# Down product of a feed-forward by seven block products instead of eight, with the second half of the tokens handed on first

## The reference

```
gate, up = jnp.split(xn @ w_gate_up[l], 2, axis=-1)
x = x + (jax.nn.silu(gate) * up) @ w_down[l]        # (1024 x 2816) @ (2816 x 1024)
return rms_norm(x, final_norm_g)
# second block, start
hc = modulate(rmsnorm(ctx, norm1_g), csh1, csc1)    # 256 context tokens
hx = modulate(rmsnorm(x, norm1_g), sh1, sc1)
q_x, k_x, v_x, ... = split(hx @ w_in)               # k_c, v_c of the context from hc
```

## Time and profile before

| | us |
|---|---|
| median of 3 runs | 3002.29 (3001.2 to 3003.21) |
| the profiled execution | 3003.17, its span 3001.1 |
| TensorE, VectorE, ScalarE, GpSimd busy in it | 2849.3, 1757.3, 1299.1, 512.4 |
| gate-up product | up to 970.6 |
| down product | 970.6 to 1212.2 |
| entry of the second block up to q | 1212.2 to some 1293 |

### The profile page before, as it was taken

How to read it: one execution, slowest core, us unless ns; L and a number is a source line. 1 busy time by engine, 2 the same in 40 slices (tenths; PEclk the granted TensorE clock), 3 DMA queues, 4 the chain that set the end, 5 groups by cost and what they waited for, 6 DMA issues and landing times.

```text
span 3001.1 us, 34761 instructions
## 1 busy us (share of the span) xinstructions
PE 2849.3 (95%) x14050; PEld 2269.2 (76%) x14050; DVE 1757.3 (59%) x2366; ACT 1299.1 (43%) x1809; POOL 512.4 (17%) x424
## 2 busy tenths in 40 slices
PE   6999998999999999899999999999999579999997
PEld 5777776788778888788888676666888368888885
DVE  4344534788775333843323555555355669999997
ACT  4344433333333223311111666665223357777775
POOL 0011102555554000421000111111000200000000
PEclk8999999999999999999999999999999789999998
DMA  3210131345654531221211111114324569999996
GB/s 106 85 43 29 43 105 71 96 137 155 189 155 152 197 102 49 84 65 43 74 60 36 50 40 43 40 43 152 102 98 169 224 224 386 398 391 398 398 397 238
DMA packets 239619, 439.79 MB, mean 147 GB/s; under 512 B 27436, under 2 KB 134068, under 8 KB 238948
## 3 DMA queue, kind: packets, MB, share of 16 engines
q1 hardware_dynamic: 217184, 359.69, 34.2%
q0 software_dynamic: 22128, 77.85, 7.5%
q10 hardware_dynamic: 148, 0.04, 0.0%
HBM read 383.96 MB, written 53.58 MB: 146 GB/s over the span
## 4 chain that ended last, share of the span: by engine, by line
PE 90%; DVE 6%; ACT 2%; issue 1%; DMA 0%; ACTq 0%; POOL 0%; POOLq 0%; DVEq 0%
PE PS L125 84%; PE PS L128 5%; DVE m L134 3%; ACT m L131 2%; DVE m L140 1%; ACT L131 0%; DVE m L176 0%; DVE m L143 0%; DVE m L179 0%; DVE m L173 0%; DMA m<-xh_scratch,small 0%; DVE m L137 0%; ACTq L182 0%; DVE small L134 0%; DMA out_dram<-m 0%
## 5 line engine op out<-in xcount | busy, mean ns | idle before, releaser
L125 PE MATMUL PS<-m,m 128*128 128x512 f32 (+4 forms) x12234 | 2662.7, 391 | 45.4 <-DVE m L134 24.2
L125 PEld LDWEIGHTS PS<-m,m 128*128 128x128 f32 (+2 forms) x12234 | 2064.9, 184 | 567.7 <-issue 121.9
L131 ACT ACTIVATE m<-m 128x2048 fp32r<-128x2048 f32 (+4 forms) x600 | 705.1, 1191 | 881.5 <-PE PS L125 507.8
L134 DVE TENSOR_TENSOR m<-m,m 128x2048 fp32r<-128x2048 f32 (+5 forms) x576 | 852.1, 1500 | 366.3 <-ACT m L131 337.3
L131 ACT ACTIVATE m<-PS 128x512 f32<-128x512 f32 (+4 forms) x503 | 279.4, 578 | 515.7 <-PE PS L125 336.4
L134 DVE TENSOR_TENSOR m<-PS,m 128x512 fp32r<-128x512 f32 (+1 forms) x360 | 235.8, 685 | 344.6 <-PE PS L125 301.1
L134 POOL TENSOR_TENSOR m<-m,m 128x512 f32<-128x512 f32 (+3 forms) x166 | 264.7, 1597 | 646.2 <-DVE small L143 208.3
L128 PE MATMUL PS<-ident,m 128*128 128x128 f32 x1592 | 225.1, 281 | 84.0 <-DVE m L149 36.0
L128 PEld LDWEIGHTS PS<-ident,m 128*128 128x128 f32 x1592 | 193.9, 145 | 122.9 <-DVE m L149 36.2
L131 ACT ACTIVATE m<-m,small 128x640 f32<-128x640 f32 (+4 forms) x199 | 156.3, 788 | 220.7 <-DVE small L137 155.2
L143 DVE CUSTOM_DVE_ANT_0 m<-PS,m 128x640 f32<-128x640 f32 (+4 forms) x192 | 146.4, 775 | 118.5 <-PE PS L125 118.5
(11 more groups left out here) (80 smaller groups left out, 451.2 us busy)
## 6 DMA issues: line engine op xcount, KB each, us to landing
m<-in_w_exp_gate_dram SPq DMA_DIRECT2D x64, 1024.0 KB, 8.6
m<-in_w_exp_up_dram SPq DMA_DIRECT2D x64, 1024.0 KB, 8.8
m<-in_w_exp_down_dram SPq DMA_DIRECT2D x64, 1024.0 KB, 8.2
m<-in_w_mod_dram SPq DMA_DIRECT2D x48, 512.0 KB, 3.7
m<-in_w_gate_up_dram SPq DMA_DIRECT2D x44, 512.0 KB, 6.4
m<-in_w_in_dram SPq DMA_DIRECT2D x41, 512.0 KB, 4.1
m<-in_w_in_dram SPq DMA_DIRECT2D x12, 1024.0 KB, 5.1
h_scratch<-m POOLq DMA_DIRECT2D x22, 512.0 KB, 3.2
```

Of the source, the lines that this page charges most:

```text
L125: return Unsent() if self.e is None else self.e.matmul(o, l, r, start=first, stop=last, **k)
L131: return Unsent() if self.e is None else self.e.activation(o, i, fn, **k)
L134: return Unsent() if self.e is None else self.e.tensor_tensor(o, a, b, op)
```

## The change

The down product is also done by seven block products. h^T is cut in A11, A12, A21, A22 (token half by hidden half) and w_down in B11 to B22 (hidden half by column half); each block product P is 11 steps of 128 hidden rows, 4 token tiles x 3 matmuls of 512 columns each, in the order P1 P2 P5 P6 P7 P4 P3. P2 adds onto P1 in the same banks and P3 onto P5.

Every step takes two pieces of 128x512, one of h and one of w. Those that are plain blocks come through two rings of eight places of 256 KB (`h_slot`, `w_slot`). The others are sums, made by GpSimd (`dn_sum`): S1 = A21 + A22, S2 = S1 - A11, S3 = A11 - A21, S4 = A12 - S2 and T1 = B12 - B11, T2 = B22 - T1, T3 = B22 - B12, T4 = T2 - B21, eleven tiles each. S1, S2, S4 live in `s_all`, T1, T2, T4 in `t_all`; A21 and B12 are first loaded there whole (2.9 MB each). S3 and T3 are made in the ring's places. The splits go to rings of four (`hs`, `ws`): both of step n wait for the matmuls of step n - 4. A place of the ring is loaded again when the split or the sum that reads it is done.

VectorE adds the results (`dn_result`) after the splits of certain steps, up to two steps past the product's end, and holds U2 and U3 in `dU2`, `dU3`; GpSimd adds U3 into x for one block. C22 and C21, the second half of the tokens, are done before P3, whose result C12 is of the first half. So the norm of tiles 4 to 7 is made during P3, and the second block's entry takes the tiles in the order 4 5 6 7 0 1 2 3 (`X_ORDER`), with the first two k2 products and four value products on the second half. The k weights of the second block are loaded early and split during P3. Loads that move: x is read back right after the gate-up's end, the rows and tables later.

```diff
+        DN_ORDER = "P1 P2 P5 P6 P7 P4 P3".split()
...
+        dU2, dU3 = ar(134, 4, 512), ar(86, 4, 512)
+        H_RING = ([("A11", t, "P1") for t in range(11)] + [(b, t, r) for t in range(11) for b, r in (("A12", "P2"), ("A22", "S1"))]
+                  + [("A11", t, "S2") for t in range(11)] + [(b, t, r) for t in range(11) for b, r in (("A11", "P7"), ("A21", "S3"))]
+                  + [("A22", t, "P4") for t in range(11)] + [("A12", t, "S4") for t in range(11)])
+        W_RING = ([("B11", t, "P1") for t in range(11)] + [("B21", t, "P2") for t in range(11)] + [("B22", t, "T2") for t in range(11)]
+                  + [(b, t, r) for t in range(11) for b, r in (("B22", "P7"), ("B12", "T3"))] + [("B21", t, "T4") for t in range(11)])
...
+        def h_ring_load(sp, j):
+            b, t, r = H_RING[j]
+            c = t + 11 * (b[2] == "2")
+            sp.wait_ge(f"h_st{c % 2}", c)
+            if j >= 8:
+                _, t_, r_ = H_RING[j - 8]
+                if r_[0] == "P":
+                    sp.wait_ge("h_low", dn_step(r_, t_), "A")
+                else:
+                    sp.wait_ge("dn_sum", r_, t_)
+            sp.dma_start(h_slot[j % 8], h_block(b, t, 1)).then_inc(*sp.landed(f"h_in{j % 8}", "d", j))
+        def w_ring_load(sp, j):
+            b, t, r = W_RING[j]
+            if j >= 8:
+                _, t_, r_ = W_RING[j - 8]
+                if r_[0] == "P":
+                    sp.wait_ge("h_low", dn_step(r_, t_), "B")
+                if r_ == "P1":
+                    sp.wait_ge("dn_sum", "T1", t_)
+                if r_[0] == "T":
+                    sp.wait_ge("dn_sum", r_, t_)
+            sp.dma_start(w_slot[j % 8], w_block(b, t, 1)).then_inc(*sp.landed(f"wd_in{j % 8}", "d", j))
...
+            sp.wait_ge("w_low", W_GU + 21)
+            for t in range(8):
+                h_ring_load(sp, t)
+                w_ring_load(sp, t)
+        def down_sp(sp):
             sp.wait_ge("gu_acc", 21, "P7")
...
+            sp.dma_start(t_all, w_block("B12", 0, 11).rearrange("(t p) n -> p t n", p=128)).then_inc(*sp.landed("ct_in"))
+            for t in range(8, 11):
+                h_ring_load(sp, t)
+                w_ring_load(sp, t)
+            for t in range(11):
+                if t == 1:
+                    sp.wait_ge("gu_acc", 21, "P4")
+                    sp.wait_ge("gu_up", 21, "C12")
+                    sp.wait_ge("h_st0", 20)
+                    sp.wait_ge("h_st1", 21)
+                    sp.dma_start(s_all, h_block("A21", 0, 11).rearrange("(t p) n -> p t n", p=128)).then_inc(*sp.landed("cs_raw"))
+                h_ring_load(sp, H_AT["P2", t])
+                w_ring_load(sp, W_AT["P2", t])
+                h_ring_load(sp, H_AT["S1", t])
+            for t in range(11):
+                h_ring_load(sp, H_AT["S2", t])
+                w_ring_load(sp, W_AT["T2", t])
+            for t in range(11):
+                h_ring_load(sp, H_AT["P7", t])
+                h_ring_load(sp, H_AT["S3", t])
+                w_ring_load(sp, W_AT["P7", t])
+                w_ring_load(sp, W_AT["T3", t])
+            for t in range(11):
+                w_ring_load(sp, W_AT["T4", t])
+                h_ring_load(sp, H_AT["P4", t])
+            for t in range(11):
+                h_ring_load(sp, H_AT["S4", t])
+                if t == 2:
+                    sp.wait_ge("dn_sum", "T4", 10)
+                    for t_ in range(4):
+                        w_last_load(sp, t_)
+                    w_load(sp, W_V2)
+            for t in range(4, 11):
+                w_last_load(sp, t)
+            sp.wait_ge("h_low", 76, "B")
+            sp.dma_start(sinT, sin_t).then_inc(*sp.landed("cs_in"))
+            sp.wait_ge("md_turned", "x", 4, 4)
+            sp.wait_ge("h2_sum", 1, 3)
             sp.dma_start(cosT, cos_t).then_inc(*sp.landed("cs_in"))
...
         def down_pe(pe):
-            for n, (c, kg, k0, kk) in enumerate(dn_pairs):
-                W = W_DN + 6 * c + kg
-                H, L = w_split(W)
-                hi, lo = hsp[n % 2]
-                pe.wait_ge("h_low", n)
-                pe.wait_ge("w_low", W)
-                for i in range(NT):
-                    if n % 11 == 0:
-                        pe.take(i, "x2_half", c, i)
-                    for k in range(2):
-                        ks = kk + k
-                        t = mm3(pe, PS[:, i, :], (hi[:, k, tile128(i)], lo[:, k, tile128(i)]), (H[:, ks, :], L[:, ks, :]),
-                                n % 11 + k == 0, k0 + ks == 21)
-                    t.then_inc(*pe.did("dn_acc", n, i))
-                    if n == 21 and i >= 3 and i < 7:
-                        _, a, k0_ = md_parts[i - 3]
+            for P in DN_ORDER:
+                added = P in ("P2", "P3")
+                for t in range(11):
+                    n = dn_step(P, t)
+                    (ah, al), (bh, bl) = hs[n % 4], ws[n % 4]
+                    pe.wait_ge("h_low", n, "B")
+                    for i in range(4):
+                        b = dn_bank(P, i)
+                        if t == 0:
+                            pe.take(b, *(("dn_s1", i) if P == "P1" else ("x2_half", DN_TAKEN[P], i)))
+                        mm3(pe, PS[:, b, :], (ah[:, tile128(i)], al[:, tile128(i)]), (bh, bl), t == 0 and not added, t == 10,
+                            **(dict(skip_group_check=True) if added else {})).then_inc(*pe.did("dn_acc", n, i))
+                    if P == "P3" and 4 <= t < 8:
+                        _, a, k0 = md_parts[t - 4]
                         pe.wait_ge("cx_shifted", a)
-                        pe.turn = i - 3
-                        turn4(pe, cx[:, a, :], k0_, 4, "md_turned", ("c", a, k0_), ("md_low", md_no["c", a, k0_]))
-                w_done[W] = ("dn_acc", n, 7)
-            pe.turn = 4
+                        pe.turn = t - 4
+                        turn4(pe, cx[:, a, :], k0, 4, "md_turned", ("c", a, k0), ("md_low", md_no["c", a, k0]))
+            pe.turn = 0
...
+        def dn_highs(act, n):
+            for x, ring in (("A", hs), ("B", ws)):
+                v, ready = dn_source(n, x)
+                act.wait_ge(*ready)
+                if n >= 4:
+                    act.wait_ge("dn_acc", n - 4, 3)
+                else:
+                    act.wait_ge("gu_acc", 21, "P1" if x == "A" else "P2")
+                act.activation(ring[n % 4][0], v, ACT.Copy).then_inc(*act.did("h_high", n, x))
+        def dn_lows(dve, n):
+            for x, ring in (("A", hs), ("B", ws)):
+                H, L = ring[n % 4]
+                dve.wait_ge("h_high", n, x)
+                dve.tensor_tensor(L, dn_source(n, x)[0], H.bitcast(F32), ALU.subtract).then_inc(*dve.did("h_low", n, x))
...
+            results = {24: "C11", 46: "U2", 48: "U2_in", 57: "U3", 58: "U3_in", 60: "C22", 69: "C21"}
+            for n in range(4, 77):
+                dn_lows(dve, n)
+                if n in results:
+                    dn_result(dve, results[n])
+                if n in (27, 29):
+                    h2_sum(dve, 0, n - 27)
+                    h2_sum(dve, 0, n - 26)
+                if n == 37:
                     dve.wait_ge("act_junk~", "cx", 1, 1)
                     dve.tensor_tensor(ssumc, ssqc[:, :, 0], ssqc[:, :, 1], ALU.add).then_inc(*dve.did("dve_order~"))
                     mean_of(dve, ssumc, 1024, "cx")
...
+                if n == 39:
                     inverse_of(dve, ssumc, rsc, "cx")
                     dve.wait_ge("rstd", "cx")
                     dve.wait_ge("crows_in")
                     for a in range(2):
                         dve.scalar_tensor_tensor(cx[:, a, :], cx[:, a, :], rsc[:, a:a + 1], cA1row, ALU.mult, ALU.mult).then_inc(
                             *dve.did("cx_scaled", a))
...
+                if n in (64, 66):
+                    h2_sum(dve, 1, n - 60)
+                    h2_sum(dve, 1, n - 59)
+                if n == 70:
+                    for i in range(4, 8):
+                        h2_sum(dve, 0, i)
+                    h2_mean(dve, 1)
+                    w_low(dve, W_K2)
+                if n == 72:
+                    h2_inverse(dve, 1)
+                    modulate_dve(dve, 4)
+                if n >= 73:
+                    md_low(dve, *md_parts[n - 73], hch, hcl)
+            modulate_dve(dve, 5)
...
+        def dn_sum(pool, S, t):
+            sv, tv = s_all[:, t, :], t_all[:, t, :]
+            if S in ("S1", "S2", "S4"):
+                j = H_AT[S, t]
+                pool.wait_ge(f"h_in{j % 8}", "d", j)
+                v = h_slot[j % 8]
+                if S == "S1":
+                    pool.wait_ge("cs_raw")
+                    pool.tensor_tensor(sv, sv, v, ALU.add).then_inc(*pool.did("dn_sum", S, t))
+                elif S == "S2":
+                    pool.wait_ge("h_low", dn_step("P5", t), "A")
+                    pool.tensor_tensor(sv, sv, v, ALU.subtract).then_inc(*pool.did("dn_sum", S, t))
+                else:
```

(50 more changed lines are left out.)

385 lines of the change are left out of this document (225 added, 160 removed), and 5 rows, old and new, of the table SHARED.

## The result

The changed kernel takes 3012.27 us (median of 13 runs, 3007.49 to 3016.16) against 3002.29 before (13 runs): ratio 1.0032, 95% interval 1.0023 to 1.0040. It is slower by 10 us; the forecast was 2988. The profiled execution has a span of 3010.5 us, 9.4 more than before.

A forecast was written before the change was run, and what follows sets the result against it. TensorE, busy for 95% of the span, bounds the kernel; the down product gains 6.0 us (29.9 of matmuls less stalls and clock), the second block's entry 8.3: 3003.2 - 14.3 = 2988.9, by the median 2988; range 2967 to 3004.

The forecast's parts named there:

- The value of a matmul and of the 132 removed: Down product: a matmul of 512 columns takes 0.2267 us, so the 132 removed are worth 29.9 us.
- one sum per split at 1.70 us: Down product: while GpSimd has sums queued, each VectorE split takes 1.70 us, a step's two 3.4 against 2.72 of matmuls.
- P6 into P7's 5.5: P6 to P7: P7's first matmul waits for U2, done only after step 46's splits, costing 5.5 us.
- the tail: Product's end to q: 69.8 us plus 2.5 of clock, with waits of 3.4 (k2's last split) and 1.9 (last split).
- P5's 6.6: P5: 22 S2 and T2 sums in step with VectorE make step 31's splits late by 6.6 us.
- The first stretch: P1 and P2: sum trains, x1's reload and A21's block ahead of step 12's pieces cost 5 us, bounds 0 and 10.
- gaps released by transfers: Down product: a sign, named beforehand, that the forecast is wrong: TensorE's gaps end with transfers; no size given.
- P7 into P4, and P3: P7 to P4: U3 behind step 57's splits 1.9 us, adding U3 0.7; P3: step 71's splits behind other work 1.9.
- The clock: Down product: the 5.5 us wait at P7 is long enough to slow TensorE's clock, costing about 2.5 us.
- The lead hides it all: Rival, down product: gaps and the four-step ring even out the sums; gain 39.7 us, 2963; chance 0.13.
- VectorE never catches up: Rival: GpSimd never dry, U2 11 us late, reload costs 10; down product 10 to 11 over forecast, 2998; chance 0.17.
- Ring latency binds: Rival, P7 and P2: pieces landing later than 4.3 us slow the steps, +24 us, 3008; chance 0.12.

The follow-up runs named there:

- e3: Changed kernel with ScalarE's copies of P1's result moved from behind step 13's splits to behind step 11's: 3008.6 us.
- e2: Changed kernel with x1's 4 MB reload and the context's load moved on GpSimd's queue behind S1's eleven sums: 3019.3 us.
- e9: Changed kernel with GpSimd's 88 sums and four U3 adds on VectorE, and start rearranged (blocks in thirds, copies earlier, x1 in three parts): 2972.0 us.
- e1: Changed kernel with GpSimd's 88 sums cut from 512 to 16 columns, so not computed; waits, loads and order stay: 2982.2 us.
- e11: Changed kernel with sums cut to 16 columns, A21 and B12 in three transfers each, x1 behind the fourth S1 sum, copies at step 11: 2970.7 us.

## Why the prediction was wrong

**Right.** The value of a matmul and of the 132 removed; the start of the product (0.4 us later, costed at nothing); one sum per split at 1.70 us; P6 into P7's 5.5 (5.6, and P7 starts with U2's first add, as said); no gap ahead of the context keys; the tail, 72.3 us forecast and 70.9 measured, with its waits of 3.4 (4.00) and 1.9 (1.57) at the places named. P5's 6.6 against 6.0 is partly luck: 1.6 of the 6.0 are slow clock behind P2's late start, and P5 itself lost 4.4.

**The first stretch: the step that failed.** The prediction put P1 and P2 at 5 us with a bound of 10; it was 15.9. It had the A21 block "ahead of step 12's pieces, which are due by 1000 and land at 1000 to 1004"; they landed at 1009.96 and 1011.91. It took the reload as a delay of B12 alone, and did not carry that on. B12 landed at 985.96; T1's first sum then frees the place of step 8's w piece, SP issues that at 987.46, it lands at 993.59, and step 8 starts with the wait of 2.83 us at 995.88. SP issues A21's block at 992.64, and the pieces of steps 12 and 13 come behind its 2.9 MB. And the prediction did not say what is queued on ScalarE behind step 13's splits: the copies that P2 waits for. e3 shows 10.9 us of P2's start for the copies (6.5 of them still gained at P5's start), e2 7.6 for the reload; with copies, reload and blocks all dealt with (e9) nothing is lost. A sum of the bytes points to it: 21.7 MB in 55 us is all that the queues carried. This is the prediction's own sign of being wrong, "gaps released by transfers", here through ScalarE's list.

**P7 into P4, and P3: two terms mis-sized.** 1.9 + 0.7, with 2.5 of clock, became 11.2 + 1.9, and 1.9 became 9.9. The mechanism was the one foreseen, VectorE held by sums; e1 removes all but 1.7 us of it. Three meetings were not priced (timelines of the kernel after, VectorE and then GpSimd; the 14 of the first row are ten splits and four adds):

```profile
1123.48 17.25 DVE L135 TENSOR_TENSOR m<-m,m 128x512 fp32r<-128x512 f32 x14 [2.49 <-ACT m L132]
...
1146.83 11.70 DVE L135 TENSOR_TENSOR m<-m,m 128x512 fp32r<-128x512 f32 x7 [0.15 <-ACT m L132]
1158.45 2.47 DVE L135 TENSOR_TENSOR m<-PS,m 128x512 f32<-128x512 f32 x4
```

```profile
1123.97 11.52 POOL L135 TENSOR_TENSOR m<-m,m 128x512 f32<-128x512 f32 x7 [0.60 <-DMA m<-in_w_down_dram]
```

Behind step 48's splits VectorE adds U2 into x, four adds with two SBUF operands each, beside seven of GpSimd's sums: they take 6.8 us from 1125.79, and step 49's splits behind them bring the wait of 2.49 us at 1136.09. GpSimd's train of 12 at 1144.84 is the last T3 and all of T4, and the prediction has no train of T4: the splits up to step 57 take 1.70 each beside it, U3 stands behind them at 1158.45, and P4 starts with its first add after 4.99 us. The train at 1180.49 is the last eight of S4 and the four adds of U3: steps 66 to 69 last 3.4 to 3.6 us (3.0 lost), and VectorE has no lead left before the heap of work behind step 70 (4.13 us and the clock).

**The clock: one wait counted, six paid.** The prediction allowed 2.5 us for one wait of 5.5. In the trace the rows behind six waits of 2.49 to 10.87 us are each too long for their count at 0.2267 and the 0.3 us that any row has over (12 matmuls show as 3.02): 10.07 for 36 (1.6 over), 50.73 for 216 (1.5), 15.45 for 60 (1.6), 18.19 for 72 (1.6), 34.81 for 144 (1.9), 5.46 for 12 (2.4). That is 10.6 us, a fifth of the 50.5 lost, and it is contained in the table's rows. The granted clock is 0.83 and 0.89 in windows that hold such rows, 1.00 from 1030 to 1060, where there is none.

**The rivals.** "The lead hides it all" (2963) fails in the kernel after, and is what e9 and e11 come close to once the sums stand elsewhere or are short. "VectorE never catches up" (2998) named the right mechanism, the reload's 10 us included, at under half the price (10 to 11 us over the forecast, where it was 26). "Ring latency binds" (3008) came nearest in time, for the wrong reason. Pieces took 5.5 us at the median, above its bound of 4.3, and GpSimd did wait for some in P7 (2.54 us ahead of 1138.03). But TensorE's waits there, at 1118.14, 1136.09 and 1159.28, each end with work that stood in VectorE's list behind held-up splits or adds, not with a landing. Late pieces held TensorE only in P1 and ahead of P2, around the blocks.
